# RWKV recurrence on one core: 64x64 products of the block inverse split into pairs of 32x32 products on diagonal tiles

## What is computed

```python
def step(S, inp):
    r_t, d_t, kk_t, a_t, k_t, v_t = inp
    sa = jnp.einsum('bhvk,bhk->bhv', S, -kk_t)
    S = S * d_t[:, :, None, :] + sa[..., None] * (kk_t * a_t)[:, :, None, :] + v_t[..., None] * k_t[:, :, None, :]
    return S, jnp.einsum('bhvk,bhk->bhv', S, r_t)
```

## Time and profile before

| what | value |
|---|---|
| median of 3 runs | 2162.68 us (2158.6 to 2167.33) |
| span of the profiled execution | 2161.5 us |
| PE busy | 2073.6 us (96%), 15204 matmul passes |
| DVE, ACT, POOL busy | 1198.2, 621.6, 168.3 us |
| 274 us stretch from 386 to 660 us, which holds the recurrence | 7400 passes, PE busy 261.5 us, DVE 183.2 us, granted clock 1.00 |

### The profile page before, as it was taken

The page is one execution under the profiler, slowest core; times in us unless marked ns, Lnnn a source line. Parts: engine busy times, 40 slices in busy tenths (PEclk is TensorE's granted clock), DMA queues, the critical chain, the costliest instruction groups (busy, mean ns, idle before and its releaser), DMA issues.

```text
span 2161.5 us, 37156 instructions
## 1 busy us (share of the span) xinstructions
PE 2073.6 (96%) x15204; PEld 1178.3 (55%) x15204; DVE 1198.2 (55%) x2401; ACT 621.6 (29%) x1401; POOL 168.3 (8%) x280
## 2 busy tenths in 40 slices
PE   8999999899998897999988999999999999999999
PEld 6445656799996784444444444444444444444443
DVE  4375644477666548776555446454454546363635
ACT  5005552222322125766644122111111111111020
POOL 3000000222222001212202000000000000000000
PEclk9999999999998998999999999999999999999999
DMA  7001113001013721000045601111111111111102
GB/s 218 0 0 30 30 30 120 33 4 23 3 24 85 203 69 56 10 6 11 1 138 176 200 0 40 39 39 39 39 39 39 39 39 39 39 39 39 41 38 83
DMA packets 96903, 115.73 MB, mean 54 GB/s; under 512 B 32251, under 2 KB 68028, under 8 KB 96670
## 3 DMA queue, kind: packets, MB, share of 16 engines
q1 hardware_dynamic: 90718, 101.82, 14.8%
q10 hardware_dynamic: 4480, 7.34, 1.2%
q0 software_dynamic: 1536, 4.20, 0.6%
HBM read 104.75 MB, written 12.64 MB: 54 GB/s over the span
## 4 chain that ended last, share of the span: by engine, by line
PE 88%; DVE 5%; ACT 4%; issue 1%; DMA 1%; ACTq 0%; SPq 0%; POOL 0%; POOLq 0%; DVEq 0%
PE psum L1413 81%; PE psum L1942 2%; PE psum L1826 1%; ACT arena L1283 1%; PE psum L1999 1%; ACT arena L1269 1%; DVE arena L2608 1%; DVE arena L2634 1%; DVE arena L2458 1%; PE psum L1744 0%; PE psum L1498 0%; SPq L790 0%; DVE psum L2605 0%; ACTq L1234 0%; PE psum L2126 0%
## 5 line engine op out<-in xcount | busy, mean ns | idle before, releaser
L1413 PE MATMUL psum<-arena 64*64 64x64 f32 (+14 forms) x12248 | 1829.7, 346 | 51.7 <-ACT arena L1283 20.2
L1413 PEld LDWEIGHTS psum<-arena 64*64 64x64 f32 (+6 forms) x12248 | 952.0, 150 | 818.1 <-issue 643.7
L2791 DVE TENSOR_TENSOR arena<-arena,psum 128x512 f32<-128x512 f32 x51 | 35.0, 687 | 318.8 <-PE psum L1413 318.8
L1386 ACT ACTIVATE arena<-psum 128x512 f32<-128x512 f32 x51 | 30.3, 594 | 437.4 <-PE psum L1413 344.8
L1375 ACT ACTIVATE arena<-arena 128x512 f32<-128x512 f32 x64 | 40.2, 628 | 274.2 <-DVE arena L2805 168.0
L935 POOL TENSOR_TENSOR arena<-arena,m_lev 128x256 f32<-128x256 f32 x82 | 65.0, 793 | 561.6 <-DVE arena L2439 363.4
L1269 ACT ACTIVATE arena<-psum 128x512 f32<-128x512 f32 (+1 forms) x148 | 80.5, 596 | 68.7 <-PE psum L1942 60.7
L2608 DVE TENSOR_REDUCE arena<-psum 128x1 f32<-128x640 f32 (+7 forms) x128 | 84.5, 702 | 14.7 <-PE psum L1413 13.2
L1283 ACT ACTIVATE arena<-psum,arena 128x640 f32<-128x640 f32 (+7 forms) x128 | 88.9, 703 | 9.5 <-DVE arena L2608 9.4
L2458 DVE TENSOR_TENSOR arena<-arena,psum 128x512 f32<-128x512 f32 x65 | 44.5, 685 | 74.2 <-PE psum L1413 73.8
L1942 PEld LDWEIGHTS psum<-ident,arena 128*128 128x128 f32 x528 | 58.1, 143 | 45.8 <-issue 22.4
(11 more groups left out here) (324 smaller groups left out, 1791.8 us busy)
## 6 DMA issues: line engine op xcount, KB each, us to landing
arena<-in_w_up_dram SPq DMA_DIRECT2D x7, 2048.0 KB, 7.5
arena<-in_w_down_dram SPq DMA_DIRECT2D x7, 2048.0 KB, 7.7
arena<-in_cache_slc_kv_dram SPq DMA_DIRECT2D x96, 128.0 KB, 2.5
arena<-in_cache_cmp_kv_dram SPq DMA_DIRECT2D x72, 128.0 KB, 3.3
arena<-in_x_prompt_dram SPq DMA_DIRECT2D x16, 512.0 KB, 12.4
arena<-in_cache_cmp_kv_dram ACTq DMA_DIRECT2D x56, 128.0 KB, 3.4
arena<-in_w_in_dram SPq DMA_DIRECT2D x13, 512.0 KB, 3.7
arena<-in_w_in_dram SPq DMA_DIRECT2D x2, 2048.0 KB, 19.2
```

Source lines behind the costliest of these rows:

```text
L1413: return nc.tensor.matmul(out, lhsT, rhs, start=start, stop=stop)
```

## The change

A new function says which blocks of a 64x64 product are computed at level i. At level index 0 and at the last level (block size 32, result blocks of 64) it gives the two halves as before. At the levels for blocks of 4, 8 and 16 (result blocks of 8, 16 and 32) everything outside the two diagonal 32x32 blocks of a head is zero, and it gives four quarters of the partitions, each with its 32 columns. So 8 products of 64x64 become 16 of 32x32 in X, 16 become 32 in T. The parts of banks 3 and 4 outside the diagonal blocks aren't written at these levels; they keep the zeros that level index 0, still computed whole, wrote there. The reads of ACT and DVE are as before.

```diff
+            def diag_blocks(i):
+
+                if i == 0 or 2 * LEVELS[i] > 32:
+                    return [(h, 0, CH) for h in HALVES]
+                return [(slice(32 * q, 32 * q + 32), 32 * (q % 2), 32) for q in range(4)]
+
             def l_pe(c, k):
...
                     for hp in range(HP):
-                        for h in HALVES:
-                            ins = mm(banks[3][h, hp * CH:(hp + 1) * CH], amt[h, n % 2, hp, :], tu[h, hp, 0, :])
+                        for r, c0, w in diag_blocks(i):
+                            ins = mm(banks[3][r, hp * CH + c0:hp * CH + c0 + w], amt[r, n % 2, hp, c0:c0 + w], tu[r, hp, 0, c0:c0 + w])
                     ins.then_inc(sem("rw_x"), 1)
...
                     for hp in range(HP):
-                        for h in HALVES:
+                        for r, c0, w in diag_blocks(i):
+                            a0 = hp * P + c0
                             if i < nlev(c) - 1:
-                                mm(banks[4][h, hp * P:hp * P + CH], tu[h, hp, 1, :], xsb[h, hp, :])
-                            ins = mm(banks[4][h, hp * P + CH:(hp + 1) * P], xsb[h, hp, :], tu[h, hp, 1, :])
+                                mm(banks[4][r, a0:a0 + w], tu[r, hp, 1, c0:c0 + w], xsb[r, hp, c0:c0 + w])
+                            ins = mm(banks[4][r, a0 + CH:a0 + CH + w], xsb[r, hp, c0:c0 + w], tu[r, hp, 1, c0:c0 + w])
                     ins.then_inc(sem("rw_tx"), 1)
```

## The result

The changed kernel takes 2191.42 us (median of 4 runs, 2188.58 to 2200.45) against 2162.62 us of the kernel before in the same session: ratio 1.0134, 95% interval 1.0107 to 1.0161. It is slower by 29 us; 2154 was forecast. The profiled execution has a span of 2187.4 us, against 2161.5.

A forecast was written before the change was run, and what follows sets the result against it. PE was taken to bound X2 to T5, PE and DVE together the rest. Full periods' 6.4 us plus 1.2, 0.7 and 0.4 elsewhere made 8.7 us, span 2161.5 to 2152.8, median 2154; range 2141 to 2186.

The forecast's parts named there:

- the sum: Array savings minus tile changes: 0.45 to 0.5 us gained per full period, 8.7 us over the kernel.
- The instructions don't come fast enough (17%), slower: Rival, 17%: PE's instruction supply can't feed small tiles, mainly in T3 and T5; +1.75 us a period, 25 us, 2187.
- 600 x 28.5 = 17.1 us is above 16.35: The supply rival's check: a period's 600 passes at 28.5 ns each would exceed the present period.
- may have been queued up: Caveat that the earlier trace's 14 ns came from 32 passes behind a wait, possibly not showing sustained supply.
- X and T: On four small tiles, X takes 0.243 us instead of 0.467 and T 0.585 instead of 0.934.
- Tile changes: Each switch drains the array: 0.12 us into 32x32 tiles, 0.145 us back to 64x64.
- DVE is full from T5 to the next X2: In this part of a period only DVE's small gaps can be gained, 0.08 to 0.15 us.
- More gained: Rival, 13%: DVE has more give and look-ahead reaches further; 1.1 us a period, 18 us, 2144.
- each start at its old cost: Rival, 4%: every pass takes 28.5 ns whatever its tile, so X 0.91 and T 1.82 us; 65 us slower, 2228.
- a slow small tile: Rival, 12%: a small tile's pass interval stays near 46 ns or above, so changes are a loss; 2169 to 2181.

The follow-up runs named there:

- the run with one level: Changed kernel with only X2 and T3 (blocks of 4) on 32x32 tiles, other levels on 64x64: 2170.83 us, ratio 1.0035 to the kernel before.
- Half of the tiles: Changed kernel computing only quarters 0 and 2, two of each product's four diagonal tiles, with all tile changes: 2159.76 us, ratio 0.9985 to the kernel before.
- T alone: Changed kernel with only the T products on small tiles at the three levels, X as before the change: 2173.53 us, ratio 1.0045.
- X alone: Changed kernel with only the X products on small tiles at the three levels, T as before the change: 2168.05 us, ratio 1.001.
- the new order: p2 and p3 alternate 64x64 tiles after every product, not three: 2159.85 us (0.9977) on the kernel before, 2191.31 (1.014) on the changed kernel.
- the long quick run: Kernel before with chunk 5's X2 issued 64 times more on four 32x32 tiles, 2048 passes: 53.5 us for these; whole kernel 2252.5 us.
- the wide run: Same execution, chunk 8's X2 issued 64 times more on 64x64 tiles, 1024 passes: no stop; whole kernel 2252.5 us.

## Why the prediction was wrong

**The step that failed** is the sum's silence on supply: it adds up what the array saves and pays, and puts the time in which PE has no instructions at nothing. The rival that had this wait ("*The instructions don't come fast enough (17%), slower*") was set aside. The runs showed in its place 1.50 us of stops a period, in a period that grew by 1.64 us. The rival's numbers, +1.75 us a period, 25 us and 2187 us, are near what was measured: +1.64 us, 29 us, 2191. That they are so near is partly luck, for it put its losses into T3 and T5 of every period, and the trace has one to five stops a period at the borders of blocks, wherever these fall. Its own check, "600 x 28.5 = 17.1 us is above 16.35", used the right figure: starved, PE got a pass each 28.5 ns on average (14 blocks of 128), each 27 ns at best. It "may have been queued up", as the text said of the 14 ns of the earlier trace rows: 32 passes are a quarter of a block, too few to show a supply. What I had wrong in it is the form, not a queue of 32 passes but blocks of 128. A view that shows this form was there: q8's packets before, 56 in 260 us, and 256 records each, one per 4.64 us. I didn't count them. How soon a starved PE gets the next block, that trace doesn't show.

**How the difference adds up.** The two profiled spans lie 25.9 us apart, and 21.3 of that is in the 13 periods from 427.15 us on. Of the 1.64 us a period, stops are 1.50, or 1.44 without the usual distance between two starts. What remains is 0.2 us more than before, where the sum had 0.46 less. An estimate of a period without any stop: in each stretch between the last passes of two products, take the shortest of the first six periods. That makes 16.17 us (16.28 before), and 16.40 in the seven periods with the four transposes of `s0_pe` (16.37 before). It is rather too low, as behind a stop the other engines have had time to catch up. So without stops next to nothing is gained or lost, and the gain that didn't come is a matter of sizes in the sum.

**X and T.** Right within 0.07 us: the 32 passes of X2 take 0.262 us between first and last start (predicted 0.243), the 64 of T3 0.657 (0.585) where no stop falls in. T7 with X6 and T7 alone on small tiles lasts 0.85 us to the end of its last pass, where the earlier trace rows and the kernel before have 1.17 and 1.20.

**Tile changes.** From the last start on one size to the first on the other, 0.120 us pass on the way back and 0.148 on the way in. The prediction's 0.145 and 0.12 are what a change costs beyond the usual distances. Measured so, the 32 passes of y4 behind X4 end their starts 1.10 us behind X4's, where 0.934 is usual: 0.165 us. And X4's starts end 0.41 us behind the large tiles' last, where its own pace makes 0.27: 0.14 us. So both are 0.02 us dearer than predicted.

But a change costs more than itself. The last passes before it run on one 64x64 tile with nothing beside them: in p2 of the run with one level the last starts lie 109 and 110 ns apart, where 52 to 57 are normal when T3 follows on the same tiles. The stretch from X2 to T3 grew by 0.36 us; by the sum (-0.224 for X2, +0.145, +0.12) it should have grown by 0.04. With only X on small tiles, T3 to X4 takes 2.50 us instead of 2.24, and T5 to X6 2.60 instead of 2.35: 0.25 us for a way in, where 0.12 was predicted. The whole follows from the shortest stretches in the changed kernel, from the transposes at k = 1 to X6's last pass: 8.65 us, against 8.40 before and 8.07 by the sum (-1.15 and -0.22 saved, +0.94, +0.12 and -0.025 paid). That is the mis-sized term: the changes and what they take from their neighbours cost 0.58 us a period more than was put down. From there to X8's last pass 0.37 us are gained, more than the 0.1 that the sum had for all from T5 on.

**DVE.** That DVE is full from T5 to the next X2 and lets PE gain only its small gaps was wrong, which is why the sum had too little there. Freeing 0.53 us at L2507 left the period at 16.33 us; what counts is DVE between T5's subtraction and T7's, where 0.50 us more made the period 0.38 us longer. Half of the tiles, with all changes and 144 passes a period fewer than the changed kernel, gain 0.28 us a period.

**Rivals.** More gained, each start at its old cost, and a slow small tile are all excluded by the rows of X2 and T3: small passes were as quick as taken.

What stays open: how much the change would take without stops. The estimate above and the periods of T alone without a stop (16.31 to 16.60) and of X alone (16.40 and 16.60), beside 16.30 and 16.38, suggest no gain; no run has the whole work with fewer instructions. With the new order the same estimate is 15.63 us, where the kernel before with that order has 16.07, so there a supply that kept up might have made the change a gain. Why a packet begins when it does is open too.

## What to carry to other kernels

Splitting a product into smaller ones multiplies PE's instructions, and these have a rate of their own: count the packets of the instruction queue in the stretch. If a block is already used up in about the time that the next one takes to come (here 3.65 us for 128 passes), what passes gain by getting quicker is mostly waited for again. Price a change of tile size with what stands before it, as the end of a run on one tile has no partner; letting the tiles take turns in that run was worth more than the small tiles. Where DVE and POOL both read two SBUF operands, a shift of 0.01 us can decide who pays 0.6 us, so look at their durations before and after any change of pace.

## What the runs showed of the hardware

- PE's instructions come by DMA in packets of 16384 bytes, 256 instructions each. A packet takes 1.1 us (0.9 to 1.5 in the changed kernel). In the long quick run it begins 1.0 to 1.15 us (once 1.5) behind the start of the block before, and its first pass starts 2.3 to 2.9 us later. A block each 3.45 us was the best there, 3.65 the average; in the changed kernel packets begin at least 3.27 us apart.
- The stops that come of it stand at exact multiples of 256 recorded PE instructions, and the profile calls them "issue".
- A starved PE can lose its clock too. In the quick run the granted clock fell to 0.50, the level of 1.2 GHz, at 480.1 us, behind a stop of 2.2 us, and stayed there while PE worked in pieces with stops (row below: busy 23.1 of 43.6 us); in the wide run, without stops, it was 1.00. In the changed kernel's 13 periods it stayed at 1.00, with stops of 1.3 us at most; with the new order it fell in two of them.

```profile
586.50:619.00 32.50, 32.50 (x1084) 32.50 (x1081) 1.92 (x4) 1.41 (x4) 1.46 (x2) 1.00 0.02 5
482.89:526.53 43.64, 23.12 (x1536) 21.56 (x1536) 0.00 (x0) 0.00 (x0) 0.00 (x0) 0.50 0.02 5
```

- Passes on four 32x32 tiles start 8.5 ns apart in X's order and 10.4 in T's, at clock 1.00.
- A no-op on PE that raises a semaphore, between matmuls, cost 147 ns all told, with a granted clock of 0.56, and 0.12 to 0.13 us by the gaps.
- A DVE multiply of 128x256 with two SBUF operands takes 1.00 us instead of 0.42 when POOL's multiply begins 0.01 us before it; POOL's takes 1.00 instead of 0.73 the other way round.
